# Expert weights as one 16 KB run per partition, with strided transposes to match, in a two-layer diffusion and MoE backbone

## What is computed

```python
def _moe(h, w_router, router_bias, w_gate, w_up, w_down):
    hf = h.reshape(-1, shp[-1])
    combine = _route(hf, w_router, router_bias)
    y = jnp.zeros_like(hf)
    for e in range(N_EXPERTS):                        # 16 experts
        a = jax.nn.silu(hf @ w_gate[e]) * (hf @ w_up[e])    # (1024, 512) each
        y = y + combine[:, e:e + 1] * (a @ w_down[e])       # (512, 1024)
```

## Time and profile before

| | value |
|---|---|
| median of 3 runs | 1906.97 us (1900.69 to 1910.23) |
| time of the profiled execution | 1905.0 us |
| span of the profiled execution | 1903.3 us |
| TensorE busy | 1703.7 us (90%), mean granted clock 0.959 |
| hardware DMA queue q1 (weights) | 160256 packets, 327.17 MB, 48.9% of 16 engines |
| software DMA queue q0 (rows, results) | 17136 packets, 66.13 MB, 9.3% |
| bytes read from HBM | 373.27 MB |

### The profile page before, as it was taken

The page is one execution under the profiler, slowest core; times in us unless marked ns, Lnnn a source line. Parts: engine busy times, 40 slices in busy tenths (PEclk is TensorE's granted clock), DMA queues, the critical chain, the costliest instruction groups (busy, mean ns, idle before and its releaser), DMA issues. The chain is left out here.

```text
span 1903.3 us, 15998 instructions
## 1 busy us (share of the span) xinstructions
PE 1703.7 (90%) x6163; PEld 760.4 (40%) x6163; DVE 464.3 (24%) x1206; ACT 339.7 (18%) x759; POOL 132.4 (7%) x219
## 2 busy tenths in 40 slices
PE   7999998889999999999989998998799949978771
PEld 1244445554444444243334324445544424422220
DVE  0323026850011124100110026307601140011002
ACT  1011027760000021000010002107600111000001
POOL 0100000110000000200000020000200010001001
PEclk9999999999999998999999999999999969988886
DMA  9971333010303044999999897334134177999993
GB/s 336 368 242 48 85 108 130 18 48 37 133 0 133 0 156 177 377 366 324 363 385 383 307 358 255 118 88 166 35 112 174 44 272 262 330 350 374 378 386 111
DMA packets 178194, 396.74 MB, mean 208 GB/s; under 512 B 23694, under 2 KB 27822, under 8 KB 177928
## 3 DMA queue, kind: packets, MB, share of 16 engines
q1 hardware_dynamic: 160256, 327.17, 48.9%
q0 software_dynamic: 17136, 66.13, 9.3%
q10 hardware_dynamic: 724, 2.38, 0.3%
HBM read 373.27 MB, written 34.18 MB: 214 GB/s over the span
## 5 line engine op out<-in xcount | busy, mean ns | idle before, releaser
L1417 PE MATMUL bank<-ring_sb,HT_sb 128*128 128x512 f32 x672 | 296.9, 597 | 2.7 <-ACT HT_sb L700 1.5
L1482 PE MATMUL bank<-ring_sb,HT_sb 128*128 128x512 f32 x576 | 253.3, 592 | 1.4 <-ACT QR_sb L791 1.4
L1417 PEld LDWEIGHTS bank<-ring_sb,HT_sb 128*128 128x128 f32 x672 | 126.2, 192 | 150.0 <-issue 148.1
L1368 PE MATMUL bank<-ring_sb,cT_sb 128*2 128x512 f32 x384 | 169.8, 603 | 2.7 <-DMA ring_sb<-w_mod 2.7
L1482 PEld LDWEIGHTS bank<-ring_sb,HT_sb 128*128 128x128 f32 x576 | 109.3, 190 | 138.7 <-issue 136.8
L1597 PE MATMUL bank<-ring_sb,QR_sb 128*64 128x512 f32 x608 | 142.7, 624 | 24.5 <-DMA ring_sb<-w_e_up 24.5
L1486 PE MATMUL bank<-ring_sb,QR_sb 128*128 128x512 f32 x288 | 129.5, 592 | 0.0
L1458 PE MATMUL bank<-WK_sb,KR_sb 128*64 128x128 f32 x960 | 68.3, 280 | 36.3 <-ACT WK_sb L801 35.5
L1613 PE MATMUL bank<-ring_sb,QR_sb 128*128 128x512 f32 x208 | 97.6, 625 | 0.0
L1583 PE MATMUL bank<-ring_sb,QR_sb 128*128 128x512 f32 x208 | 94.1, 606 | 3.4 <-ACT QR_sb L837 3.4
L1590 PE MATMUL bank<-ring_sb,QR_sb 128*128 128x512 f32 x208 | 91.4, 592 | 0.0
(11 more groups left out here) (209 smaller groups left out, 1377.3 us busy)
## 6 DMA issues: line engine op xcount, KB each, us to landing
ring_sb<-w_e_gate SPq DMA_DIRECT2D x32, 2048.0 KB, 10.1
ring_sb<-w_e_up SPq DMA_DIRECT2D x32, 2048.0 KB, 15.1
ring_sb<-w_e_down SPq DMA_DIRECT2D x32, 2048.0 KB, 12.5
ring_sb<-w_mod SPq DMA_DIRECT2D x24, 2048.0 KB, 12.9
ring_sb<-w_in SPq DMA_DIRECT2D x22, 2048.0 KB, 15.1
MB_sb<-mod_d POOLq DMA_DIRECT2D x16, 512.0 KB, 8.0
ring_sb<-w_branch SPq DMA_DIRECT2D x8, 1024.0 KB, 9.9
ring_sb<-w_out SPq DMA_DIRECT2D x4, 2048.0 KB, 10.5
```

The source lines that it names most:

```text
L1368: ins = mm(bank[use][0:2, :], cT[:, k, :], WR[slot][:, k], start=(k == 0), stop=(k == KD - 1))
L1417: ins = mm(bank[j % 4][:, :], HT[:, k, P * t:P * t + P], WR[slot][:, k], start=(k == 0), stop=(k == KD - 1))
L1482: ins = mm(bank[i % 2][:, :], HT[:, k, P * t:P * t + P], WR[wg][:, k], start=(k == 0), stop=(k == KD - 1))
```

## The change

`expert_source` now arranges the rows as `(p k) n -> p k n`. Partition p takes 8 consecutive rows of a gate or up matrix, or 4 consecutive rows of a down matrix: one run of 16 KB in HBM. To match, block k of the transposed rows must hold columns k, k+8, k+16 and so on of `hg`, and block k of the transposed product columns k, k+4 and so on of `ea`. The new helper `spread` reads these columns with a stride of 8 or 4 floats. It takes the place of `rows_of` and of `transposes` in the expert stage. The number of transposes, their shapes and everything that follows are as before.

```diff
             def expert_source(l, e, j):
...
-                return w.rearrange("(k p) n -> p k n", p=P)
+                return w.rearrange("(p k) n -> p k n", p=P)
...
-                def rows_of(src, q, dst, count):
-                    if full_rows(l, q):
-                        return transposes(src, dst, count)
+                def spread(src, rows, dst, count, first=0, parts=None):
+
+                    by_k = src.rearrange("q (p k) -> q k p", k=parts or count)
                     for k in range(count):
-                        ins = mm(dst[:, HALF * k:HALF * k + HALF], src[0:HALF, P * k:P * k + P],
-                                 ident[0:HALF, 0:HALF], start=True, stop=True, is_transpose=True)
+                        ins = mm(dst[:, rows * k:rows * k + rows], by_k[0:rows, first + k], ident[0:rows, 0:rows],
+                                 start=True, stop=True, is_transpose=True)
                     return ins
...
                     if full_rows(l, q):
                         for g in range(2):
-                            ins = transposes(hg[q % 2][:, CW * g:CW * g + CW], bank[6 + g], 4)
+                            ins = spread(hg[q % 2], P, bank[6 + g], 4, 4 * g, KD)
                     else:
-                        ins = rows_of(hg[q % 2], q, bank[6], KD)
+                        ins = spread(hg[q % 2], HALF, bank[6], KD)
...
-                    rows_of(ea, q, bank[2], 4).then_inc(ea_tr, 1)
+                    spread(ea, P if full_rows(l, q) else HALF, bank[2], 4).then_inc(ea_tr, 1)
```

More of the change, by code:

```diff
@@ L1656, in _ @@
                         for g in range(2):
-                            ins = transposes(hg[0][:, CW * g:CW * g + CW], bank[6 + g], 4)
+                            ins = spread(hg[0], P, bank[6 + g], 4, 4 * g, KD)
                         ins.then_inc(q["hg_tr"], 1)
@@ L1665, in _ @@
                         eng.wait_ge(q["a"], n + 1)
-                        transposes(ea, bank[3], 4).then_inc(q["a_tr"], 1)
+                        spread(ea, P, bank[3], 4).then_inc(q["a_tr"], 1)
                         eng.wait_ge(q["aT"], n + 1)
```

## The result

The changed kernel takes 1959.24 us (median of 4, 1951.89 to 1963.46), the kernel before 1906.06 beside it. The ratio is 1.0271, with an interval of 1.0234 to 1.0309: slower by 2.7%, where 0.7% faster was forecast. 1959 lies outside the range too.

The account below looks back on a forecast made before the run. It took DMA (the fuller) and TensorE as bounding layer 0, TensorE layer 1's full experts, DMA its half experts. Terms -5, +2.7, -10, -1 gave -13.3 us: 1893.7 us against the median, range 1874 to 1921.

Parts of the forecast that it names:

- The price of a packet: Weight loads: 9.5 ns fixed per packet, 610 ns at 16 KB, 430 GB/s; an expert's weights take 1.28 us less.
- The stride: Expert transposes: strided reads double the 53 ns weight load, costing 0.64 us an expert, 1.27 us a pair.
- What bounds layer 0: Layer 0's steady pairs, 37.4 us: DMA and TensorE both nearly full, DMA the fuller.
- 2.6 us less DMA per pair: Layer 0's pairs: larger packets cut the DMA time needed from 37.4 to 34.9 us.
- The row load: Layer 0's rows beside 16 KB weight packets: only 1 or 2 packets meet weights; wait set at 1.5 us.
- If every packet met a weight packet: Layer 0's stores and row load: 12 packets an engine add 5.4 us, raising the 3.24 us wait to 8.6.
- case (d): Row loads starve behind a weight backlog: pairs 44 us, half experts 17.5, +35 us in all; chance 0.05.
- The half experts of layer 1: DMA-bound ten periods of 17.0 us fall to 15.9 to 16.3, about 1.0 us each: -10 us.
- Layer 0: Layer 0's experts: -2 from steady pairs, -5 from shorter waits, +1.9 for the first three experts: -5 us.
- layer 1's full experts: First 4 or 5 experts of layer 1, TensorE-bound: no gain from packets, strided transposes cost +2.7 us.
- The gap ahead of layer 1: Before layer 1's experts, 19.01 us: five matrices finish earlier and half may reach the row scatter, -1 us.

Follow-up runs that it names:

- early rows: Row load issued one expert earlier: on the kernel before, 1876.59 us (ratio 0.9850); on the changed kernel, 1882.70 us (0.9881).
- both cures: Changed kernel with row load issued one expert earlier and each layer's first two experts read in 2 and 4 KB packets: 1867.99 us, ratio 0.9813.
- the strides alone: Changed kernel with the loads of before (2 and 4 KB packets), keeping only the strided transposes: 1919.03 us, ratio 1.0058.
- the 4 KB version: Kernel before with gate and up rows taken in pairs (4 KB runs), transposes at every second float: 1914.03 us; with early rows 1871.83 us.

## Why the prediction was wrong

**The price of a packet: right.** It forecast 425 to 435 GB/s in pure weight traffic. The queue of the changed kernel in 976:980:

```profile
DMA packets 123, 1.74 MB, mean 435 GB/s; under 512 B 16, under 2 KB 16, under 8 KB 17
...
q1 hardware_dynamic: 121, 1.74, 101.4%
```

101.4% of 16 x 4 us over the 105 large ones is 0.62 us a packet, where 610 ns were worked out. The gain in the DMA-bound stage was sized nearly right as well, once nothing else stood in its way: about 1.0 us a half expert was forecast, 17.0 to between 15.9 and 16.3, and 0.8 to 0.9 was measured between the kernels with early rows (17.1 to 16.3, and 16.2 with both cures). That needed two changes that the forecast did not have.

**The stride: right in the mean, wrong in its form.** The weight loads rose from 138 and 141 ns to 203, where about 190 were forecast. (The spacings 115 and 80 ns that the prediction used leave 45 ns for the contiguous load and not 53; this changes little.) But the doubling of 53 ns did not fall on every transpose. Eight transposes of 64 rows now keep the next group waiting 1.02 us instead of 0.64, 48 ns each. With 128 rows it is 0.99 us for 0.93 in the two runs with early rows, 8 ns each: the extra 62 ns of the weight load hide behind 128 streamed columns. So the working's sentence that the load "is not hidden" held for 64 rows only, and a pair pays 0.8 us (34.8 for 34.0 between the same two runs), not 1.27. What the strides alone did cost, 11 us at a ratio of 1.0058, was more than their 4.5 us in layer 0: busy time there rose by 9.1 us over the earlier trace rows (223.88 for 214.75), and the rest of it came with a mean granted clock of 0.94 for 0.96. Why the clock was lower at nearly the same waits was not tried.

**What bounds layer 0: wrong for what sets the time, right for how close the DMA stood.** The prediction read a DMA share of 1.03 at 375 GB/s as "the fuller" of two bounds, took the 37.4 us of a pair for the DMA's own time and gave it 34.9 after the change. With early rows and the old packets the twelve experts take 208.80 us for 236.20, at TensorE's 34.0 a pair. So 37.4 was not the DMA's time; the 3.24 us of the earlier trace rows was the latency of one load issued late. Of the 27.4 us that went, 21.4 were the row waits of the kernel before, and 7.2 are busy time (207.55 for 214.75) that came back with the full clock; a wait of 1.2 us for an up matrix is new.

But the DMA did not keep up with that pace. One pair of it, and the weight queue over the twelve experts, both in the kernel before with early rows:

```profile
983.05:1017.09 34.04, 34.04 (x122) 14.36 (x120) 3.77 (x6) 3.47 (x7) 2.70 (x5) 1.00 1.04 387
...
q1 hardware_dynamic: 28983, 69.83, 90.4%
```

Twelve experts use 36 matrices, 75.5 MB. Only 69.8 came in that time (75.9 in the same stretch of the kernel before); the rest had been loaded ahead into the slots, and a load of an up matrix landed 20.9 us after its issue for 12.6. A pair needs 14.0 MB, which at 387 to 392 GB/s is about 36 us, an estimate: more than TensorE's 34.0, less than 37.4. For these twelve experts "2.6 us less DMA per pair" would have been worth almost nothing and the row load's latency nearly everything. In a longer stage without row waits the DMA would set the pace at 2 KB, while at 16 KB and early rows it delivers 406 GB/s beside pairs of 34.8 and keeps up; no run here has such a stage.

**The row load: the step that failed.** The prediction worked out the right number and then gave it up. "If every packet met a weight packet" the wait would grow to 8.6 us; measured 7.70. The full case (d), pairs of 44 us and half experts of 17.5, got 0.05; measured 44.1 and 18.4, and its own sign, waits of 6 us or more, is what the profile shows. How near 8.6 came is partly luck, since it let every packet meet a weight packet, and most packets of q0 passed in 970.5:973 beside few; only the engines that finished last come near that case. Two sentences argued it away. The first had the weight queue empty when the rows come, with only one or two packets meeting. In fact the up matrix issued at 957.79 still had the gate matrix of 951.07 ahead of it and landed at 969.2, down landed at 975.1, and the first packets of q0 ran just after 967, ahead of both. The second said that weights "can't have such a backlog when pairs last 44 us but need 35 of DMA". That is an average over a pair. The changed kernel in four stretches of 2 us from one pair (in 986:988, behind the last, the share is 0.00):

```profile
968.00:970.00 2.00, 2.00 (x10) 0.43 (x6) 0.00 (x0) 0.00 (x0) 0.00 (x0) 1.00 1.02 432
...
972.00:974.00 2.00, 0.00 (x0) 0.00 (x0) 0.00 (x0) 0.00 (x0) 0.00 (x0) 1.00 0.98 352
...
978.00:980.00 2.00, 2.00 (x9) 1.86 (x9) 0.00 (x0) 0.23 (x1) 0.00 (x0) 0.50 1.05 451
...
984.00:986.00 2.00, 2.00 (x6) 0.90 (x5) 0.69 (x1) 0.00 (x0) 0.00 (x0) 1.00 0.04 16
```

The spare time is there, but behind the row load; while the row load is in flight the engines are full. Weights and rows are released by the same products, so they always come together; a queue whose engines are idle for a seventh of the time can still be full at each moment that matters. The account by busy time of the twelve experts agrees: 29.3 us more is 20.4 of longer row waits (41.8 for 21.4), 4.5 of stride (its price with early rows), and 4.4 left over, which goes with a granted clock of 0.92 for 0.96.

**The half experts of layer 1** failed by the same step. "With the queue partly empty" the period was put at 15.9 to 16.3 us; it became 18.4, above even the worst case of 17.5. The idle time there now has one cause, 43.1 us for rows; before, 24.5 us were for the up weights and 12.6 for rows.

**The start: not seen.** 13.6 us, more than the whole forecast gain, came from a scatter that the prediction mentioned only ahead of layer 1, where it expected a gain of 1 us. It had looked only at the stretches of the two expert stages. The weights of the first two experts are prefetched long before, beside whatever runs there.

**The sum.** Layer 0 was put at -5 and came to +43 with its start, layer 1's full experts at +2.7 and came to +1.3, its half experts at -10 and came to +13.5 over eleven periods. The gap ahead of layer 1 was put at -1 and came to -1.07. Why the scatter there got faster beside 16 KB packets while the one of layer 0 got slower was not looked into.

## What to carry to other kernels

A larger descriptor on one queue is a longer turn for every other queue that shares its engines. Before packets are made larger, list the small, latency-bound transfers that run beside them in the whole trace, from prefetch on, and price each at its number of packets per engine times the new packet's time, without assuming an empty queue; average shares say nothing about that. Before a share is called a limit or no limit, compare the bytes that came in a stretch with the bytes that it used: buffers filled ahead can hide a queue that falls behind. And where a wait for a short load stands on the critical path, first ask what its issue waits for: moving that one line here was worth 1.5%, and the larger packets brought at most 0.4% on top of it.

## What the hardware showed

Where two queues both had work, they took turns by packet whatever the sizes: 924 to 1022 packets in 13 us at 4 KB against 2, 770 to 744 in 27 us at 4 KB against a mean of 12. A DMA share a little over 1 said that the engines were nearly full, not that they set the time: 1.03 stood beside 375 GB/s and pairs of 37.4 us, 1.04 beside 387 to 392 GB/s and pairs of 34.0 that lived partly on weights loaded ahead. A weight load of a transpose that reads every fourth or eighth float took 203 ns at the median, and one of every second float no less (214 to 220 in two groups of eight of the 4 KB version), where contiguous ones took 138 to 141; behind 128 streamed columns nearly all of that was hidden.
